# Second mixer: norms per unit, heads in pipelined order, and two value units placed within the heads

## The reference, cut to what matters

```python
def fox_attention(h, w_in, b_f, q_norm_g, k_norm_g, w_out):
    proj = h @ w_in                                   # 1024 -> 4*1024 + 16
    q = rmsnorm(proj[..., :FOX_D].reshape(bsz, s_len, FOX_HEADS, FOX_HEAD_DIM), q_norm_g)
    k = rmsnorm(proj[..., FOX_D:2 * FOX_D].reshape(bsz, s_len, FOX_HEADS, FOX_HEAD_DIM), k_norm_g)
    v = proj[..., 2 * FOX_D:3 * FOX_D].reshape(bsz, s_len, FOX_HEADS, FOX_HEAD_DIM)
    gate = proj[..., 3 * FOX_D:4 * FOX_D]
    log_f = jax.nn.log_sigmoid((proj[..., 4 * FOX_D:] + b_f).astype(jnp.float32))
    cum = jnp.transpose(jnp.cumsum(log_f, axis=1), (0, 2, 1))
    ...
        sc = jnp.einsum('bhqd,bhkd->bhqk', q[:, :, qs:qe], k[:, :, :qe]).astype(jnp.float32) * scale
        sc = sc + cum[:, :, qs:qe, None] - cum[:, :, None, :qe]
        mask = (qs + jnp.arange(Q_BLOCK))[:, None] >= jnp.arange(qe)[None, :]
        p = jax.nn.softmax(jnp.where(mask, sc, -jnp.inf), axis=-1)
        outs.append(jnp.einsum('bhqk,bhkd->bhqd', p.astype(v.dtype), v[:, :, :qe]))
    ...
    return (o * jax.nn.sigmoid(gate)) @ w_out
```

## Time and profile before

| | |
|---|---|
| three runs | 1905.51, 1908.0, 1915.07 us |
| median | 1908.0 us |
| the profiled execution: run | 1914.68 us |
| the profiled execution: span of the trace | 1912.9 us |
| busy: TensorE | 1764.0 us, 92% |
| busy: VectorE | 1125.3 us, 59% |
| busy: GpSimd | 912.9 us, 48% |
| busy: ScalarE | 817.7 us, 43% |
| HBM traffic | 310.84 MB, mean 162 GB/s |

### The profile page before, as it was taken

How to read it: one execution, slowest core, us unless ns; L and a number is a source line. 1 busy time by engine, 2 the same in 40 slices (tenths; PEclk the granted TensorE clock), 3 DMA queues, 4 the chain that set the end, 5 groups by cost and what they waited for, 6 DMA issues and landing times. The chain is left out here.

```text
span 1912.9 us, 34813 instructions
## 1 busy us (share of the span) xinstructions
PE 1764.0 (92%) x12587; PEld 1650.5 (86%) x12587; DVE 1125.3 (59%) x2114; ACT 817.7 (43%) x1102; POOL 912.9 (48%) x268
## 2 busy tenths in 40 slices
PE   5889999999987899999796999979999999999996
PEld 5879899999986799999566899979999988888885
DVE  5767854335293354444786694465555367777775
ACT  3556434335543343335242544534444443333332
POOL 3644557887680048887401288876666610000000
PEclk9989999999995599999897999989999999999998
DMA  4332345555450025555201166645455587777774
GB/s 176 133 132 89 111 141 182 184 177 189 155 186 22 1 89 195 179 197 205 88 23 45 58 214 235 213 150 187 169 180 177 182 269 237 239 238 236 239 237 142
DMA packets 77436, 310.84 MB, mean 162 GB/s; under 512 B 8752, under 2 KB 10288, under 8 KB 60720
## 3 DMA queue, kind: packets, MB, share of 16 engines
q1 hardware_dynamic: 74288, 304.64, 47.8%
q10 hardware_dynamic: 3072, 5.15, 0.8%
HBM read 290.89 MB, written 18.87 MB: 162 GB/s over the span
## 5 line engine op out<-in xcount | busy, mean ns | idle before, releaser
L715 POOL TENSOR_TENSOR lo<-raw,hi 128x2048 fp32r<-128x2048 f32 x128 | 589.6, 4618 | 484.2 <-ACT hi L556 410.8
L338 PE MATMUL ps<-xh,hi 128*128 128x256 f32 (+1 forms) x1984 | 569.5, 287 | 39.3 <-POOL lo L715 22.3
L340 PE MATMUL ps<-xh,lo 128*128 128x256 f32 (+1 forms) x1984 | 560.7, 283 | 0.0
L339 PE MATMUL ps<-xl,hi 128*128 128x256 f32 (+1 forms) x1984 | 560.7, 283 | 0.0
L338 PEld LDWEIGHTS ps<-xh,hi 128*128 128x128 f32 x1984 | 378.8, 191 | 43.1 <-issue 31.5
L737 POOL TENSOR_TENSOR lo<-raw,hi 128x1024 fp32r<-128x1024 f32 x128 | 321.0, 2532 | 139.1 <-ACT hi L1641 139.1
L340 PEld LDWEIGHTS ps<-xh,lo 128*128 128x128 f32 x1984 | 378.4, 191 | 0.0
L339 PEld LDWEIGHTS ps<-xl,hi 128*128 128x128 f32 x1984 | 377.6, 190 | 0.2
L1641 ACT ACTIVATE hi<-raw 128x1024 fp32r<-128x1024 f32 x256 | 264.6, 1057 | 214.6 <-PE ps L340 204.8
L2280 DVE TENSOR_TENSOR lo<-raw,hi 128x1024 fp32r<-128x1024 f32 x128 | 156.3, 1222 | 86.4 <-ACT hi L1641 86.3
L338 PE MATMUL ps<-hi,wgh 128*128 128x512 f32 x512 | 201.1, 393 | 1.5 <-DVE wgl L2291 1.5
(11 more groups left out here) (445 smaller groups left out, 3302.9 us busy)
## 6 DMA issues: line engine op xcount, KB each, us to landing
raw<-in_w_u SPq DMA_DIRECT2D x128, 512.0 KB, 4.3
raw<-in_w_v SPq DMA_DIRECT2D x128, 512.0 KB, 4.2
raw<-in_w_up SPq DMA_DIRECT2D x44, 1024.0 KB, 4.7
raw<-in_w_down SPq DMA_DIRECT2D x22, 1024.0 KB, 4.8
raw<-in_w_fox SPq DMA_DIRECT2D x16, 1024.0 KB, 4.9
act_save<-act_out SPq DMA_DIRECT2D x64, 256.0 KB, 2.0
act_in<-act_save SPq DMA_DIRECT2D x64, 256.0 KB, 3.2
raw<-in_w_xbc SPq DMA_DIRECT2D x12, 1024.0 KB, 4.9
```

The costliest lines, as they stand in the source:

```text
L338: pe.matmul(o, ah, bh, start=start, stop=False)
L339: pe.matmul(o, ah, bl, start=False, stop=False)
L340: return pe.matmul(o, al, bh, start=False, stop=stop)
L715: return g.tensor_tensor(lo[slot][:], raw[slot][:], hi[slot][:].bitcast(F32), ALU.subtract)
```

## The change

The q and k norms are made unit by unit, the heads follow in another order, and the last two of the value units move into the heads.

- **Order of units** (`FOX_ORDER`): the gate's four, q, k, then v. Positions 0 to 13 run ahead of the heads on TensorE; the third and fourth value unit (positions 14 and 15) are worked through by `late_values` after turn_p(4) and after turn_p(8). Value heads 8 to 11 and 12 to 15 are in them.
- **Norms**: for each q or k unit ScalarE writes the squares to PSUM (banks 2 and 3); VectorE reduces them there, takes the inverse square root in twelve small operations on 8 columns, which alternate between `rs` in SBUF and bank 4 of PSUM so that each has an operand in PSUM, and multiplies the unit's bank directly into `fq` or `fk` (signal `qk_norm`). TensorE waits for it before it reuses the bank. The gains of q and k and the factor 1/8 are one column, `gqk`, which ScalarE applies to the turned q (two activations of 256 columns instead of one of 512).
- **Log1p and cum**: the operations get operands in PSUM; the matmuls of the cumulative sum come after unit position 6, its copy after the fourth norm.
- **Heads**: turn(0) ahead of position 13, turn(1) and scores(0) in the middle of it, and then per head scores(n + 1), turn(n + 2), turn_p(n), the placed unit if n is 4 or 8, values(n - 1). ScalarE evacuates and splits after a placed unit at its head 5 and 9, between the turned copies and the diagonals.
- **Output**: the first two fills (banks 0 and 1) precede the last head's values; each fill waits for its own four heads' gated result (`o_gated`).

```diff
         ffn(0, U_FFN0)
-        run(U_FQ, "w_fox", range(16))
+        run(U_FQ, "w_fox", FOX_ORDER)
...
+            def first_heads():
+                pe.wait_ge(b_evac, 5)
+                turn(1)
+                scores(0)
+
+            def late_values(n):
                 unit_wait(pe, U_FQ + n)
-                if n >= 2:
+                pe.wait_ge(b_evac, n - 8)
+                pe_b(pe, (U_FQ + n) % RING, [(ps[:, 1, t * 256:(t + 1) * 256], META + t * P, P) for t in range(NT)])
+
+            for n in range(14):
+                unit_wait(pe, U_FQ + n)
+                if 2 <= n < 6:
                     pe.wait_ge(b_evac, n - 1)
+                elif n >= 6:
+                    pe.wait_ge(qk_norm, n - 5)
+                if n == 13:
+                    pe.wait_ge(qk_norm, 8)
+                    turn(0)
...
+            for n in range(H):
+                if n + 1 < H:
+                    scores(n + 1)
+                if n + 2 < H:
+                    turn(n + 2)
+                if n % 4 == 1 or n == 0:
+                    pe.wait_ge(b_evac, (6, 6, 7, 8)[n // 4])
+                turn_p(n)
+                if n in (4, 8):
+                    late_values(14 + (n - 4) // 4)
+                if n >= 1:
+                    values(n - 1)
+            pe.wait_ge(t_evac, H)
+            fill(0)
+            fill(1)
+            values(H - 1)
+            out_unit(0)
...
+            for n in range(14):
+                if n == 13:
+                    turned(0)
+                    turned(1)
+                evacuate(n)
...
+            for n in range(FH):
                 exps(n)
+                if n + 2 < FH:
+                    turned(n + 2)
+                if n in (5, 9):
+                    evacuate(14 + (n - 5) // 4)
                 for k in range(2 * n, min(2 * n + 2, CONV_K)):
...
+            for q in range(8):
+                dst, part = (fq, fk)[q // 4], q % 4
...
+                v.wait_ge(q_squares, q + 1)
+                sig_v(v.tensor_reduce(eight(0), ps[:, 2 + q % 2, :].rearrange("p (t a b) -> p t a b", t=2, a=4), AX.X, ALU.add), b_sq)
+                ch(v.tensor_scalar(rs[:, 0, 0:8], ps[:, 4, 0:8], 1.0 / HD, EPS, ALU.mult, ALU.add))
+                rsqrt(v, ch, ps[:, 4, 32:40], None, HD, rs[:, 0, 0:8], ps[:, 4, 16:24], rs[:, 1, 0:8])
+                ch(v.tensor_tensor(r8, eight(32), bc(rc[:, 0:NT], 2, [P, NT, 4]), ALU.mult))
+                sig_v(v.tensor_tensor(dst[:, :, 4 * part:4 * part + 4, 0:HD], ps[:, q % 2, :].rearrange("p (t a b) -> p t a b", t=2, a=4),
+                                      r8.unsqueeze(3).broadcast_to([P, NT, 4, HD]), ALU.mult), qk_norm)
...
-            for kind, (dst, gain) in enumerate(((fq, "fqg"), (fk, "fkg"))):
-                r = stat[:, 16 + 32 * kind:48 + 32 * kind]
-                rsqrt(v, ch, r, r, HD)
-                if kind == 0:
-                    ch(v.tensor_scalar(r, r, HD ** -0.5, None, ALU.mult))
-                rv = r.rearrange("p (a b) -> p a b", a=2)
                 for t in range(NT):
-                    d = dst[:, t, :, 0:HD]
-                    ch(v.tensor_tensor(d, d, bc(rv[:, t, :], 2, [P, FH, HD]), ALU.mult))
-                    ch(v.tensor_tensor(d, d, bc(RH(gain, HD), 1, [P, FH, HD]), ALU.mult))
-            chain_mark(v, qk_ready)
...
```

More of the change, by code:

```diff
@@ L354, in pe_a, with pe_b @@
         m.then_inc(unit_used, 1)
[L356 removed]
+    def pe_b(pe, s, outs, width=256, ready=None, middle=None):
         wh, wl = cv3(hi[s][:]), cv3(lo[s][:])
         for i, (o, c, m_) in enumerate(outs):
+            if middle is not None and i == 1:
+                middle()
             for k in range(KC):
@@ L526, in pe_out, with out_split @@
             pe.wait_ge(o_ready, done0 + n + 1)
-            pe_w(pe, (u0 + n) % RING, oh[:, n % 2], ol[:, n % 2], n == 0, n == nv - 1, groups and n == 0)
-    def out_split(v, n, gain, u0, done0):
+            pe_w(pe, (u0 + n) % RING, oh[:, n % 2], ol[:, n % 2], n == 0, n == nv - 1, (y_added, 8) if n == 0 else None)
+    def out_split(v, n, gain, u0, done0, bank=2):
         v.wait_ge(o_filled, done0 + n + 1)
@@ L980, in fox, with fill, out_unit @@
                     pe.matmul(ps[:, 5, FH:2 * FH], tri[:], fst[:, 2, 1, :], start=False, stop=True).then_inc(cum_mm, 1)
-            pe.wait_ge(b_evac, 16)
-            pe.wait_ge(qk_ready, 1)
-            attention()
-            pe.wait_ge(attn_ready, 1)
-            pe_out(pe, xn, 4, U_FOUT, 8)
+            def fill(n):
+                pe.wait_ge(o_gated, n + 1)
+                if n >= 2:
+                    pe.wait_ge(o_ready, 8 + n - 1)
+                for kk in range(2):
+                    for t in range(NT):
+                        c = (2 * n + kk) * P
+                        m = pe.transpose(ps[:, n % 2, (kk * 2 + t) * P:(kk * 2 + t + 1) * P], xn[:, t, c:c + P], ident[:])
+                m.then_inc(o_filled, 1)
+            def out_unit(n):
+                unit_wait(pe, U_FOUT + n)
+                pe.wait_ge(o_ready, 8 + n + 1)
+                pe_w(pe, (U_FOUT + n) % RING, oh[:, n % 2], ol[:, n % 2], n == 0, n == 3, (o_evac, 4) if n == 0 else None)
+            for n in range(H):
[15 more added lines that the diff above has]
+            out_unit(0)
+            for n in range(1, 4):
+                if n + 1 < 4:
+                    fill(n + 1)
+                out_unit(n)
         def mla():
@@ L1998, in fox @@
-            chain_mark(v, qk_ready)
-            v.wait_ge(b_evac, 16)
-            attention(stat[:, 32:128], xn, fg)
-            dve_out(v, 4, None, U_FOUT, 8)
+            pair = lambda c: ps[:, 6, c:c + 2 * FH].rearrange("p (a b) -> p a b", a=2)
+            v.wait_ge(h_kept, 8)
+            v.wait_ge(f_mm, 1)
+            for t in range(NT):
+                ins = v.scalar_tensor_tensor(pair(32)[:, t, :], ps[:, 3, 64 + t * FH:64 + (t + 1) * FH], rc[:, t:t + 1], RH("bf", FH), ALU.mult, ALU.add)
@@ new lines, in outs @@
+            def outs(q):
+                v.wait_ge(o_mm, 4 * q + 4)
+                b = 6 + q % 2
+                sm = st[:, 16 + 8 * q:16 + 8 * q + 8]
+                ch(v.reciprocal(sm, sm))
+                for t in range(NT):
+                    o = xn[:, t, q * 256:(q + 1) * 256]
+                    ins = v.tensor_tensor(o.rearrange("p (a b) -> p a b", a=4), ps[:, b, t * 256:(t + 1) * 256].rearrange("p (a b) -> p a b", a=4),
+                                          sm.rearrange("p (a b) -> p b a", b=2)[:, t, :].unsqueeze(2).broadcast_to([P, 4, HD]), ALU.mult)
+                sig_v(ins, o_evac)
+                for t in range(NT):
+                    o = xn[:, t, q * 256:(q + 1) * 256]
+                    ins = v.tensor_tensor(o, o, fg[:, t, q * 256:(q + 1) * 256], ALU.mult)
+                sig_v(ins, o_gated)
@@ new lines, in fox @@
+            maxes(0)
+            for n in range(H):
+                if n + 1 < H:
+                    maxes(n + 1)
+                turned(n)
+                if n % 4 == 1 and n >= 5:
+                    outs(n // 4 - 1)
+                if n == 3:
+                    meta_split()
+            out_split(v, 0, None, U_FOUT, 8, 0)
+            out_split(v, 1, None, U_FOUT, 8, 0)
+            outs(3)
+            out_split(v, 2, None, U_FOUT, 8, 0)
+            out_split(v, 3, None, U_FOUT, 8, 0)
```

264 lines of the change are left out of this document (113 added, 151 removed).

## The result

| | before | changed |
|---|---|---|
| median of four runs | 1911.53 us | 1862.75 us |
| lowest to highest | 1905.51 to 1916.14 | 1860.2 to 1866.49 |
| span of the profiled execution | 1912.9 us | 1858.8 us |
| ratio | | 0.9751, 95% interval 0.9729 to 0.9773 |

A forecast was written before the change was run, and what follows sets the result against it. It took the second mixer's heads as bound by TensorE at half clock after a 12.2 us norms wait. The 116.4 us stretch, summed to 90.8 and chosen as 84, less 2.0 moved, saves 30.4: 1877 us, range 1855 to 1893.

The forecast's parts named there:

- theory A: Second mixer's heads: clock falls at the seam and after at least one placed unit; stretch 80 to 91, 1873 to 1885; chance 0.52.
- B: Clock falls once at most, or the first placed unit restores it for good; stretch 66 to 76, 1860 to 1870; chance 0.20.
- seam: After position 13 ScalarE evacuates, splits, loads Exp and does two exponentials: 5.0 us, 3.7 idle on TensorE, clock fall likely.
- heads 0 to 4: Heads ahead of the first placed unit, all at half clock: 4 × 4.62 = 18.5 us.
- restart: Behind each placed unit TensorE's 2.0 us, then ScalarE's chain to the next probabilities: 7.7 us, some 3 idle.
- heads 10 to 15: Heads after the second restart, at half clock: 21.4 us.
- work moved into position 13: Two turns and one head's scores placed inside the last unit ahead of the heads: 2.0 us, taken off the saving.
- Norms per unit: Eight q and k units: VectorE 3.75 us each, under TensorE's 5.68; no GpSimd stalls, and the 12.2 us wait goes.
- The placed units: Two value units within the heads: 8.0 us each; they fill no TensorE gap, cost their length and make a gap.
- the clock in the heads: Heads taken at half clock, 4.62 us each, about 2.65 at full; three head periods of 2.2 us allowed to run fast.
- D: A, with VectorE's gate multiplies and meta operations caught by GpSimd's splits in the heads: +8 to +18, 1885 to 1895; chance 0.13.
- F: Norm chain of q and k units caught by GpSimd, one 4.5 us wait per chain: 1898, with two waits 1934; chance 0.05.

The follow-up runs named there:

- all units in front: The changed kernel with the two placed value units back ahead of the heads, first turns and scores inside position 15: 1856.71 us, 0.9715 of before.
- filler run: The kernel before with 100 matmuls that nobody reads added in TensorE's 12.2 us wait for the norms: 1910.38 us, ratio 0.9994.
- the run with old heads: The kernel before with norms per unit, all 16 units in front and the old order of heads kept: 1898.12 us, 0.9921 of before.
- the run that brings the collision about: The changed kernel with ScalarE's split behind each placed unit moved ahead of the turned copies: 1858.99 us, 0.9743 of before.

## Why the prediction was right, and where it was off

Right: faster, by more than a measurement of this kernel can tell from no change; the falls of the clock that theory A named; and what each edit does. The range held, but by its width: theory A's own sum was 1873 to 1885, and the time came where B's sum lay, for another reason than B's. The terms of the sum against the trace of the changed kernel, from the end of position 13:

| term | forecast | measured |
|---|---|---|
| seam | 5.0 | 5.4 |
| heads 0 to 4 | 18.5 | 11.1 |
| transposition and first placed unit | 8.65 | 6.1 |
| restart | 7.7 | 7.2 |
| heads 6 to 8 | 9.2 | 8.8 |
| transposition and second placed unit | 8.65 | 6.8 |
| restart | 7.7 | 7.2 |
| heads 10 to 15 | 21.4 | 13.6 |
| tail | 4 | 3.3 |
| sum | 90.8, chosen 84 | 69.5 |

The sum of 90.8 takes 21.4 for heads 10 to 15, where five periods of 4.62 are 23.1, and gives no reason. And the 2.0 us of work moved into position 13 don't follow from the terms given, 0.44 twice and 0.9 less 0.3, which are 1.5; position 13 took 7.5 us (543.94 to 551.42) in place of 5.68, so 1.8 more.

**Norms per unit**: right. The wait went, 3.8 us per chain (3.75 forecast), no stall. **The seam**: right, 3.93 us of idle (3.7) and a fall of the clock behind it. **The restarts**: right in size and cause, twice 2.61 us of idle (about 3), and the runs with ScalarE's work moved show that it was this work. **The placed units** fill no gap: right; with no idle stretch left they are worth nothing measurable, and as placed here they cost 7 us.

**The step that failed** is the clock in the heads. I wrote that heads alone never brought it back in 90 us, and gave them the half-clock period for that reason. That row was of the old order, in which each head waits for its own exponentials. In the new order the clock came back some 4 us into the heads in the changed kernel, 10 us with all units in front, and 14 us behind a 10 us idle stretch. Only heads 6 to 8 ran at 0.50 as forecast (8.8 us against 9.2): there the clock came back within the second placed unit. Of the 21.3 us between 90.8 and 69.5 two terms hold 15.2: heads 0 to 4 (7.4 us) and heads 10 to 15 (7.8); the placed units hold 4.4, since the first ran at full clock throughout and the second for all but its first microsecond, where 8.0 was taken for each; the 6.6 us that I took off for heads at full clock were too few. The third mixer's rows were the better witness, since they showed the new order holding 1.00; I used them for the price at full clock and for rival B, not for the forecast. And B's own mechanism, one fall at most or a return for good, didn't occur either: the clock fell three times and came back three times. By the profiled spans the miss is 23.7 us (54.1 against 30.4): 14.5 between the marks, 0.2 in where the first one lies, 4.7 ahead of them, where 2.0 more had been forecast and 2.7 less were measured, which is spread, and 4.3 behind them, of which the forecast had nothing.

**The reading of the bound** was half right. I took the 12.2 us wait as what had brought the clock down, and so as the cause of slow heads. The filler run and the run with old heads show otherwise: with the wait filled or gone the old order runs at 0.50 for most of its length. By the ratios the norms per unit bring 15 us (the wait, and an earlier start of the output), the new order 39, placing −7. What in the old order keeps the clock down is settled in part. Where it had come back, in the filler run, it fell behind the 2.57 us of idle of each fourth head, which the new order doesn't have. What holds it at 0.50 through the other heads isn't settled: TensorE is idle for about a tenth of each, in one piece, but in the filler run it came back at 616 with just such idle pieces. For these heads the traces show that the two orders differ, not why.

**D** didn't come about by a margin of 0.9 us; the run that brings the collision about has no longer gap for it. **F** is real where the chain has no PSUM operand, 28 us.

## What to carry to other kernels

An order in which TensorE doesn't wait for its own head's exponentials was worth more here than the waits it hides: a head fell from 5.1 to 2.5 us, some 1.6 by the clock and 1.0 by the order (each fourth head aside). Before placing dense work inside a chain of small steps, look at what it issues on the other engines: its evacuation and the next split belong beside it or behind the exponentials, not between the turned copies and them. A clock row read off one order of work is no evidence for another.

## What the runs showed of the hardware that I had not expected

The clock fell behind an idle stretch of 2.61 us (0.50 from 582 to 590), and in the filler run of the old order behind 2.57. The length of the last idle stretch alone doesn't tell: with all units in front it fell at the tail behind 0.37 and 1.05 us (0.62 over 612 to 616), and with 0.34 and 1.07 in the changed kernel it didn't. It came back in heads of small matmuls with no unit among them, some 4, 10 and 14 us into them in three runs. The same matmuls in the old order, with a wait of 0.61 us in each head, stayed at 0.50 for 80 us in one execution, and came back after 34 us in the filler run. And an operation of eight elements per partition took up to 4.58 us on VectorE with its operands all in SBUF and GpSimd in a split.
